# A pooled branch's output projection computed as seven half-size products, with its weight differences formed by GpSimd

## The reference, cut to what matters

```
u_a, z_a, q, k, v, o, z_b, gates, g_a, g_b = split(rms_norm(x) @ w_in)
mixed = groupwise(multiscale_pool(u_a)) @ pool_mix_w       # 4 groups of 256
y_a   = (mixed * pool_scale) * silu(z_a)                   # 512 x 1024
p_a   = y_a @ w_proj_pool                                  # 512 x 1024 x 1024, the product changed
merged = sigmoid(g_a + b_merge[0]) * p_a + sigmoid(g_b + b_merge[1]) * p_b
```

## Time and profile before

| | us |
|---|---|
| median of 3 runs (lowest, highest) | 1134.78 (1134.07, 1134.80) |
| the profiled execution's own time | 1134.12 |
| its span, first to last instruction | 1132.3 |
| TensorE busy | 1126.3 (99%), 6090 matmuls |
| VectorE busy | 724.7 (64%) |
| ScalarE busy | 614.6 (54%) |
| GpSimd busy | 197.0 (17%) |
| granted TensorE clock | 1.00 throughout |

### The profile page before, as it was taken

How to read it: one execution, slowest core, us unless ns; L and a number is a source line. 1 busy time by engine, 2 the same in 40 slices (tenths; PEclk the granted TensorE clock), 3 DMA queues, 4 the chain that set the end, 5 groups by cost and what they waited for, 6 DMA issues and landing times.

```text
span 1132.3 us, 15715 instructions
## 1 busy us (share of the span) xinstructions
PE 1126.3 (99%) x6090; PEld 935.0 (83%) x6090; DVE 724.7 (64%) x1222; ACT 614.6 (54%) x1062; POOL 197.0 (17%) x193
## 2 busy tenths in 40 slices
PE   9999999999999999999999999999999999999998
PEld 7888888888888888888889888777888888877877
DVE  5584534599845776534558667667786575666786
ACT  5533431243436676634246677777545587577752
POOL 1000135440000000000000002643503000706530
PEclk9999999999999999999999999999999999999999
DMA  6423476673331212233255523231254233222431
GB/s 195 133 75 112 124 247 233 218 244 100 122 112 57 93 58 73 76 127 112 75 204 156 130 86 76 74 92 58 95 186 132 76 111 104 75 75 76 147 124 74
DMA packets 115026, 134.13 MB, mean 118 GB/s; under 512 B 18620, under 2 KB 93756, under 8 KB 113416
## 3 DMA queue, kind: packets, MB, share of 16 engines
q1 hardware_dynamic: 113720, 128.93, 35.9%
q10 hardware_dynamic: 1232, 4.19, 1.0%
HBM read 120.37 MB, written 12.74 MB: 118 GB/s over the span
## 4 chain that ended last, share of the span: by engine, by line
PE 98%; ACT 1%; DMA 0%; DVE 0%; issue 0%; DVEq 0%; ACTq 0%
PE acc L2052 22%; PE acc L2053 22%; PE acc L2054 22%; PE aux L2052 3%; PE aux L2054 3%; PE aux L2053 3%; PE aux L2538 3%; PE aux L2526 3%; PE acc L2502 3%; PE acc L2451 2%; PE acc L2453 2%; PE acc L2452 2%; PE aux L2284 1%; PE aux L2286 1%; PE aux L2285 1%; PE aux L2144 1%
## 5 line engine op out<-in xcount | busy, mean ns | idle before, releaser
L2052 PE MATMUL acc<-ht_hi,whi 128*128 128x512 f32 x712 | 278.1, 391 | 0.0
L2054 PE MATMUL acc<-ht_hi,wlo 128*128 128x512 f32 x712 | 277.1, 389 | 0.0
L2053 PE MATMUL acc<-ht_lo,whi 128*128 128x512 f32 x712 | 277.1, 389 | 0.0
L1406 DVE TENSOR_TENSOR wlo<-raw,whi 128x2048 fp32r<-128x2048 f32 x68 | 159.5, 2346 | 101.8 <-ACT whi L951 95.6
L951 ACT ACTIVATE whi<-raw 128x2048 fp32r<-128x2048 f32 x68 | 129.9, 1910 | 56.8 <-DMA raw<-w_in_dram 22.1
L2052 PEld LDWEIGHTS acc<-ht_hi,whi 128*128 128x128 f32 x712 | 133.7, 188 | 28.1 <-DVE wlo L1406 0.6
L2054 PEld LDWEIGHTS acc<-ht_hi,wlo 128*128 128x128 f32 x712 | 133.6, 188 | 27.9
L2053 PEld LDWEIGHTS acc<-ht_lo,whi 128*128 128x128 f32 x712 | 133.7, 188 | 27.1
L848 POOL TENSOR_SCALAR whi<-raw 128x512 fp32r<-128x512 f32 x52 | 39.5, 760 | 621.9 <-DMA raw<-e_w_in_dram 464.6
L2052 PE MATMUL acc<-whi,ht_hi 128*128 128x512 f32 (+1 forms) x224 | 83.9, 375 | 0.0
L2054 PE MATMUL acc<-whi,ht_lo 128*128 128x512 f32 (+1 forms) x224 | 83.8, 374 | 0.0
(11 more groups left out here) (344 smaller groups left out, 2160.5 us busy)
## 6 DMA issues: line engine op xcount, KB each, us to landing
raw<-w_in_dram SPq DMA_DIRECT2D x72, 512.0 KB, 4.6
raw<-o_w_in_dram SPq DMA_DIRECT2D x28, 512.0 KB, 4.7
weight_terms<-term_parts SPq DMA_DIRECT2D x8, 1024.0 KB, 4.8
raw<-e_w_in_dram SPq DMA_DIRECT2D x14, 512.0 KB, 5.2
raw<-w_proj_pool_dram SPq DMA_DIRECT2D x8, 512.0 KB, 4.0
term_parts<-o_w_out_dram SPq DMA_DIRECT2D x8, 512.0 KB, 6.4
raw<-w_proj_mlstm_dram SPq DMA_DIRECT2D x8, 512.0 KB, 4.1
raw<-w_out_dram SPq DMA_DIRECT2D x8, 512.0 KB, 4.4
```

The costliest lines, as they stand in the source:

```text
L1406: v.tensor_tensor(wlo[:, slot, :], raw[:, slot, :], whi[:, slot, :].bitcast(F32), ALU.subtract).then_inc(w_split, 1)
L2052: mm(out_, w_hi_, x_hi, start=first, stop=False)
L2053: mm(out_, w_hi_, x_lo, start=False, stop=False)
L2054: return mm(out_, w_lo_, x_hi, start=False, stop=last)
```

## The change

The product p_a is computed by a seven-product scheme on halves: the contraction and the output channels are halved on the weights' side (blocks b11, b12, b21, b22 of 512x512) and the tokens and the contraction on the operand's side (`early` and `late` 256 tokens, tiles 0 to 3 and 4 to 7). The four weights T1 to T4 are differences of blocks, four subtractions by GpSimd per 128 rows, four batches; they are loaded, made and stored to DRAM while SyncE issues the loads of the za stage, and come back as one DMA of a megabyte each. The four operands' sums are made by VectorE with ScalarE during the ga stage. The stage has seven units, each of two banks by two groups by four tiles by three matmuls of 256 columns, in PSUM banks that keep partial sums from one unit to the next; ScalarE copies three of the partial results, VectorE adds them to others and multiplies by the gates. The loads and stores of the eight batches for the last projections move as well: the i of `between_loads` now counts from the first ga load, and the positions are given by `LOAD_AFTER`: batch 0 is loaded behind the load of ga's third unit, 1 behind the fourth, 2 behind pa's first; the store of batch 1 stands ahead of pa's second load, and the store of batch 2 ahead of its third (A12_B21); the other five batches stand between the loads of qk.

```diff
--- before.py
+++ after.py
@@ the Block's set-up @@
+        pool_weight_parts = at("pool_weight_parts", [P, 2, 4, WIDE], R4)
+        pool_terms_dram = nc.dram_tensor("pool_weight_terms", (4, P, 4, WIDE), F32, kind="Internal").ap()
...
-        for name, units, accs in (("gates", 1, 1), ("u", 4, 4), ("za", 4, 4), ("mix", 1, 4), ("ga", 4, 4), ("pa", 4, 4),
+        for name, units, accs in (("gates", 1, 1), ("u", 4, 4), ("za", 4, 4), ("mix", 1, 4), ("ga", 4, 4), ("pa", 7, 2),
...
+        POOL_OPERANDS = {A11_B11: (op_hi[:, 0:4, early], op_lo[:, 0:4, early]), S3_T3: (op_hi[:, 0:4, late], op_lo[:, 0:4, late]),
+                         A12_B21: (op_hi[:, 4:KT, early], op_lo[:, 4:KT, early]), S2_T2: (pool_sum_hi[1], pool_sum_lo[1]),
+                         S1_T1: (pool_sum_hi[0], pool_sum_lo[0]), S4_B22: (mix_parts[:, 0:4, early], mix_parts[:, 4:KT, early]),
+                         A22_T4: (op_hi[:, 4:KT, late], op_lo[:, 4:KT, late])}
+        def pool_bank(u, b):
+
+            if u == A12_B21:
+                return aux[:, b, :]
+            return acc[:, 2 * ((POOL_A + (u in (S3_T3, A22_T4))) % 2) + b, :]
@@ sync @@
-            stage("za", W1, COL_ZA)
+            pool_view = wview(A["w_proj_pool"][0])
+
+            def load_pool_parts(k):
+                if k == 0:
+                    sp.wait_ge(tr_lo, KT)
+                if k >= 2:
+                    sp.wait_ge(pool_terms_out[k % 2], 16)
+                for q, rows in ((0, k), (2, 4 + k)):
+                    sp.dma_start(pool_weight_parts[:, k % 2, q:q + 2, :].rearrange("p q c -> p (q c)"),
+                                 pool_view[:, rows, :]).then_inc(pool_parts_in[k % 2], 16)
+
+            def store_pool_terms(k):
+                sp.wait_ge(pool_terms_made, k + 1)
+                sp.dma_start(pool_terms_dram[:, :, k, :].rearrange("q p c -> p q c"),
+                             pool_weight_parts[:, k % 2, :, :]).then_inc(pool_terms_out[k % 2], 16)
+            for u in range(4):
+                load(W1, COL_ZA + u * UC, plan["za"][0] + u)
+                if u:
+                    store_pool_terms(u - 1)
+                load_pool_parts(u)
...
+            store_pool_terms(3)
...
+            LOAD_AFTER = (2, 3, 4, 11, 12, 14, 15, 17)
+
             def between_loads(i):
                 for b in range(len(BATCHES)):
-                    if 3 * b // 2 == i:
+                    if LOAD_AFTER[b] + 1 == i:
+                        store_terms(b)
+                for b in range(len(BATCHES)):
+                    if LOAD_AFTER[b] == i:
                         load_parts(b)
-                for b in range(len(BATCHES)):
-                    if 3 * b // 2 + 1 == i:
-                        store_terms(b)
-            stage("ga", W1, COL_GA)
-            between_loads(0)
             for u in range(4):
-                load(wview(A["w_proj_pool"][0]), u * UC, plan["pa"][0] + u)
-                between_loads(1 + u)
+                load(W1, COL_GA + u * UC, plan["ga"][0] + u)
+                between_loads(u)
+
+            def pool_term_weights(u, q):
+                n = POOL_N + u
+                slot_free(n)
+                sp.dma_start(raw[:, n % SLOTS, :], pool_terms_dram[q].rearrange("p k c -> p (k c)")).then_inc(w_loaded[n % SLOTS], 16)
+            load_wide(pool_view, 0, POOL_N + A11_B11, 0)
+            between_loads(4)
+            for stored_ in pool_terms_out:
+                sp.wait_ge(stored_, 32)
+            pool_term_weights(S3_T3, T3)
+            between_loads(5)
+            load_wide(pool_view, 0, POOL_N + A12_B21, 1)
+            pool_term_weights(S2_T2, T2)
+            pool_term_weights(S1_T1, T1)
+            load_wide(pool_view, WIDE, POOL_N + S4_B22, 1)
+            pool_term_weights(A22_T4, T4)
...
-                between_loads(5 + u)
+                between_loads(11 + u)
@@ gpsimd, ahead of the eight batches of term_parts @@
+            for k in range(4):
+                pool.wait_ge(pool_parts_in[k % 2], 32 * (k // 2 + 1))
+                b11, b12, b21, b22 = (pool_weight_parts[:, k % 2, q, :] for q in range(4))
+                step(nc.gpsimd.tensor_tensor(b11, b12, b11, ALU.subtract))
+                step(nc.gpsimd.tensor_tensor(b12, b22, b12, ALU.subtract))
+                step(nc.gpsimd.tensor_tensor(b22, b22, b11, ALU.subtract))
+                nc.gpsimd.tensor_tensor(b21, b21, b22, ALU.subtract).then_inc(pool_terms_made, 1)
@@ scalar @@
-                head(mixT[:, j, :], op_hi[:, j, :])
+                head(mixT[:, j, mix_cols(j)], op_hi[:, j, mix_cols(j)])
...
+            def heads_of_sums(u):
+                if u == 1:
+                    for m, (src, hi) in enumerate(((pool_sum_raw[0], pool_sum_hi[0]), (pool_sum_raw[1], pool_sum_hi[1]),
+                                                   (mixT[:, 0:4, late], op_hi[:, 0:4, late]),
+                                                   (mixT[:, 4:KT, early], mix_parts[:, 0:4, early]))):
+                        act.wait_ge(pool_sum, m + 1)
+                        nc.scalar.activation(hi[:, :, :], src[:, :, :], ACT.Copy).then_inc(pool_sum_high, 1)
+            stage("ga", mergedT, ACT.Sigmoid, ("b_merge", 0), heads_of_sums)
...
+            weight_heads(n0 + A12_B21)
+
+            def copies_of_term(u, part):
+                for b in range(2):
+                    act.wait_ge(pool_term, 2 * u + b + 1)
+                    nc.scalar.activation(pool_part[part][:, b, :], pool_bank(u, b), ACT.Copy).then_inc(pool_copied, 1)
+            copies_of_term(A11_B11, 0)
+            weight_heads(n0 + S2_T2)
+            copies_of_term(S3_T3, 1)
+            weight_heads(n0 + S1_T1)
+            copies_of_term(S2_T2, 2)
@@ vector @@
+            (a11, a21), (a12, a22) = ((mixT[:, tiles, early], mixT[:, tiles, late]) for tiles in (slice(0, 4), slice(4, KT)))
+            v.tensor_tensor(pool_sum_raw[0][:], a21, a22, ALU.add).then_inc(pool_sum, 1)
+            dve.wait_ge(pool_sum, 1)
+            v.tensor_tensor(pool_sum_raw[1][:], pool_sum_raw[0][:], a11, ALU.subtract).then_inc(pool_sum, 1)
+            v.tensor_tensor(a21, a11, a21, ALU.subtract).then_inc(pool_sum, 1)
+            dve.wait_ge(pool_sum, 3)
+            v.tensor_tensor(a12, a12, pool_sum_raw[1][:], ALU.subtract).then_inc(pool_sum, 1)
             weight_rests(n0 + 3)
+            for m, (src, hi, lo) in enumerate(((pool_sum_raw[0][:], pool_sum_hi[0][:], pool_sum_lo[0][:]),
+                                               (pool_sum_raw[1][:], pool_sum_hi[1][:], pool_sum_lo[1][:]),
+                                               (a21, op_hi[:, 0:4, late], op_lo[:, 0:4, late]),
+                                               (a12, mix_parts[:, 0:4, early], mix_parts[:, 4:KT, early]))):
+                dve.wait_ge(pool_sum_high, m + 1)
+                v.tensor_tensor(lo, src, hi.bitcast(F32), ALU.subtract).then_inc(pool_sum_split, 1)
...
+            weight_rests(n0 + S2_T2)
+            for b in range(2):
+                dve.wait_ge(pool_term, 2 * A12_B21 + b + 1)
+                ins, tiles = added(A12_B21, b, 0, 0)
+                step(ins)
+                gated(gates_of(0, early, b), tiles)
+            weight_rests(n0 + S4_B22)
+            for b in range(2):
+                dve.wait_ge(pool_term, 2 * S1_T1 + b + 1)
+                ins, tiles = added(S1_T1, b, 1, 1)
+                ins.then_inc(pool_added, 1)
+                dve.wait_ge(pool_added, b + 1)
+                gated(gates_of(1, late, b), tiles)
+            weight_rests(n0 + A22_T4)
+            for b in range(2):
+                dve.wait_ge(acc_ready, 2 * a0 + b + 1)
+                ins = gated(gates_of(1, early, b), two_tiles(pool_bank(S4_B22, b)))
+            ins.then_inc(acc_free, 1)
+            weight_rests(n0 + units)
...
@@ tensor @@
-            stage("pa", by_channels, op_hi, op_lo)
+
+            def pool_product(u, b):
+                slot, (hi, lo), bank = (POOL_N + u) % SLOTS, POOL_OPERANDS[u], pool_bank(u, b)
+                opens = u in (A11_B11, S3_T3, A12_B21)
+                for m in range(2):
+                    out_ = bank[:, UC * m:UC * m + UC]
+                    for k in range(4):
+                        c = WIDE * k + P * (2 * b + m)
+                        w_hi_, w_lo_ = whi[:, slot, c:c + P], wlo[:, slot, c:c + P]
+                        mm(out_, w_hi_, hi[:, k, :], start=opens and m == 0 and k == 0, stop=False, skip_group_check=True)
+                        mm(out_, w_hi_, lo[:, k, :], start=False, stop=False, skip_group_check=True)
+                        ins = mm(out_, w_lo_, hi[:, k, :], start=False, stop=m == 1 and k == 3, skip_group_check=True)
+                ins.then_inc(acc_ready if u in (S4_B22, A22_T4) else pool_term, 1)
+            for u in range(7):
+                wait_split(pe, POOL_N + u)
+                for b in range(2):
+                    if b == 0:
+                        if u == A11_B11:
+                            pe.wait_ge(acc_free, POOL_A - 1)
```

(57 more changed lines are left out.)

21 lines of the change are left out of this document (19 added, 2 removed).

## The result

| | before | after |
|---|---|---|
| time, median of 6 runs each on the same chip | 1134.78 us (1134.07 to 1135.28) | **1151.91 us** (1151.63 to 1152.87) |
| ratio to before, 95% interval | | 1.0155 [1.0144, 1.0166] |
| span of the profiled execution | 1132.3 | 1149.8 |

What follows compares the result with a forecast made beforehand. The prediction took TensorE, 98% of the chain, to bound the kernel. Its terms, -3.3 (product) + 4.0 (za) + 5.9 (queue) + 0.3 (rest of pa) + 1.5 (qk) = +8.4, gave 1142.6 us; interval 1132 to 1150.

Steps and rivals of the forecast that it cites:

- The product: In pa: 336 matmuls of 256 columns at 0.1198 us take 40.25 us against 43.52, so -3.3 us.
- The port in u and za: In u and za: GpSimd's subtractions delay VectorE, pausing TensorE 3.2 and 0.8 us; +4.0, bounds 0.9 to 7.
- SyncE's queue: At pa's third unit: its load stands behind waits for GpSimd's subtractions; pause of 5.9 us, bounds no pause to 9.8.
- qk: In the qk stage: more batches meet the convolutions and use up VectorE's margin; +1.5 us, between 0 and 4.8.
- The rest of pa: In pa's later units: loading and splitting fit their slots, except 0.3 us at S4_B22, the tightest.
- The fourth: In u, queue and qk: every subtraction holds VectorE for its full 1.29 us; +16, 1150 us, chance 0.10.
- Rivals 1 to 3: Subtractions fit gaps: 1131 to 1131.9, chance 0.13; queue absorbs u's delay: 1135.6, 0.09; u escapes, queue does not: 1138.0, 0.08.
- The fifth: In pa: wide weight loads fail to hide at 256 columns, so the stage isn't shorter; given no chance of its own.

Runs made afterwards that it cites:

- e3: Changed kernel without GpSimd's sixteen subtractions for the pooled projection and its 32 for the last two projections, transfers kept: 1130.86 us, ratio to before 0.9969.
- e1: Changed kernel without GpSimd's sixteen subtractions for the pooled projection's weights, loads and stores kept: 1145.56 us, ratio to before 1.0099.
- q1: Changed kernel, nothing left out, with T3's load moved ahead of batch 1's store and batch 2's load, and batch 2's store behind T2's load: 1143.81 us.
- p2: Kernel before the change with thirteen scratch additions on VectorE ahead of the weight rest of ga's last unit: 1145.41 us, ratio 1.0098.
- e2: Changed kernel without GpSimd's 32 subtractions of the eight batches for the last two projections, loads and stores kept: 1137.49 us, ratio to before 1.0028.
- p1: Kernel before the change with eight scratch additions on VectorE ahead of the weight rest of ga's last unit: 1136.67 us, ratio 1.0021.
- q2: Changed kernel with the pooled projection's subtractions begun after the third za unit's split, stores issued by GpSimd, parts 2 and 3 loaded behind ga's first load: 1146.01 us.
- q6: q4 with the eight batches' loads moved back near their places before the change, and batch 3 behind pa's last load: 1135.11 us, ratio to before 1.0007.
- q4: Changed kernel with pooled subtractions begun after the third za split, GpSimd issuing its own stores, and the eight batches spread over ga, pa and qk loads: 1137.03 us.

## Why the prediction was partly right

**The product: right.** -3.3 was forecast, from 336 x 0.1198 = 40.25; e3 lasts 40.31 and gains 3.4.

**The port in u and za: right in its mechanism and its length.** Forecast were no pause at the first za unit, 3.2 at the second and 0.8 at the third; the trace has 0.4, 3.45 and 1.0. What it left out is the lower clock behind the second pause, 1.8. The times hold as well: GpSimd started at 49.95 (49.4 forecast) and 65.29 (64.5), the second unit's rest ended at 77.05 (76.25). e1 showed that nothing but the subtractions was behind it, and VectorE's timeline that it was VectorE they delayed.

**SyncE's queue: right in its mechanism, near in its size.** The chain came much as written: from load to store it took 15.9, 17.2 and 13.8 us where 15.0, 16.6 and 16.1 were forecast, and the load of A12_B21 5.7 us into pa where 6.5 was forecast. From its load to its split that unit took 12.4 us (173.04 to 185.48) where 10.9 was taken from the earlier trace rows, since the transfer landed later. Its lateness was 6.65 us for 5.9 forecast. S3_T3's late megabyte made a pause of its own, 2.2 where "may be a microsecond late" was written, but it lay inside A12_B21's time, as the prediction said. This is read from the trace; no run takes away one of the two pauses alone. q1 showed that the order of the queue is behind both: 8.1 us. The upper bound was summed wrong: cycles of 16.1, 18.5 and 18 give a pause of 10.8 by the prediction's own terms, not 9.8, and three cycles may be no longer than 13.9 for no pause, not 14.2.

**A term was missing: the clock behind a pause.** "Any pause of TensorE that the change brings is lost in full" was as far as I went. In the trace three of the pauses have 5.0 us of slow matmuls behind them, and p2 shows the same in the kernel before. Of the 5.0, the 1.6 behind S3_T3's pause passed inside the wait for A12_B21, so 3.4 reached the span. Which pauses it falls behind is not fixed either: in e1 and q1 it falls behind qk's third pause too, where after has it at 1.00.

**qk: mis-sized, outside its bound.** This is the largest miss. 1.5 was forecast with 4.8 as the upper end; it measured 5.5 in four pauses and 5.8 from qk's start to the scores (e2 and q1 leave 6.3, with a fall of the clock in q1). The reason for taking little, "a TensorE already late gives VectorE time as well", did not hold. The reading of it, which no run tests, is that SyncE issues the batches behind slots that TensorE frees, so they are late with it and meet the same operations. VectorE's timeline shows two of the ways:

```profile
236.13 2.30 DVE L1514 TENSOR_TENSOR wlo<-raw,whi 128x2048 fp32r<-128x2048 f32 x1 [3.74 <-ACT whi L1036]
...
262.18 5.86 DVE L1740 SCALAR_TENSOR_TENSOR cacc<-cpad,vecs,cacc 128x512 f32<-128x512 f32 x4
...
272.55 2.28 DVE L1514 TENSOR_TENSOR wlo<-raw,whi 128x2048 fp32r<-128x2048 f32 x1
```

Ahead of the first pause VectorE was idle for 3.74: there the weights were late, their load standing in SyncE's queue behind a wait for GpSimd. Ahead of the rest at 272.55 it was not idle, and four of its operations took 5.86 where the earlier trace rows has 3.11 for four alone: the port. I had counted only the second way. How the 5.8 divide between the two was not measured. In the waits, SyncE (before 300 us) waits for GpSimd:

```profile
SPq L740 <- POOL term_parts L972: 85.7, 8, 13.9
SPq L707 <- POOL pool_weight_parts L965: 34.3, 4, 10.9
```

**The rest of pa** (0.3 at S4_B22) did not show.

**The sum as it should have been:** -3.2 + 4.9 (za) + 1.8 (clock in za) + 6.65 (A12_B21) + 1.6 (clock behind it) + 5.8 (qk) = +17.5, the span's own +17.5. Against the forecast's terms, qk is 4.3 too small, the clock's 3.4 are absent, za's and the queue's lengths are 0.9 and 0.75 too small, and the 0.3 did not come. The range was narrower than its own terms: all upper bounds together, as written, are -3.3 + 7 + 9.8 + 0.3 + 4.8 = +18.6, or 1152.7.

**The rivals.** The fourth, the fully locked port, comes nearest in time (1150), but not in its terms: it put the second za pause at 6.5, where 3.45 was measured, and cycles of 18 in the queue, where 15.9, 17.2 and 13.8 were. Rivals 1 to 3 each needed one of the two costs to be absent; both are there. The fifth fell with pa's 0.12 us.

## What to carry to other kernels

Where a saturated TensorE is given a pause, price the pause and what the clock may do behind it: here 1.6 to 1.8 us more behind each of three, and hardly anything behind six shorter ones, at 1.91 us and less of idle time. Then ask what the next unit waits for: slow matmuls ahead of a unit that is late by itself cost nothing, as those behind S3_T3's pause did. A store that waits for another engine's result, in the queue that also issues the loads, puts every load behind it at that engine's mercy; moving two calls was worth 8.1 of 17.1 us. Work on GpSimd is free only at its place: the same 32 subtractions cost at most some 0.5 us before and 14 after, so before moving such work, look at what VectorE does there and how much it has to spare.

## What the runs showed of the hardware

- The clock fell behind all eleven pauses of weight rests with 2.06 us or more of idle time in the profiled executions here (the shortest at 168.55 in e1, the longest p2's 9.16), and behind none with 1.72 (p1) or less. In between, length does not decide: it fell behind 1.86 (q2), 1.89 (q1) and 1.92 (e1) and stayed at 1.00 behind 1.89 (q6), 1.91 (after) and 1.95 (q4). Executions of the same kernel differ as well: q6 has five at a mean of 1.000 and six at 0.998, which are 1.8 us longer by their medians. What decides was not tested.
- While the clock is low, matmuls of 256 columns start 0.213 us apart instead of 0.12, and those of 512 columns 0.427 instead of 0.227 (after, from 177.13 and from 78.12).
- A VectorE operation of 16 elements took 1.15 us beside a GpSimd subtraction (51.95 to 53.10; GpSimd's lasted from 51.43 to 53.06), so the delay goes with GpSimd's instruction and not with the size of VectorE's. The Trainium skill (SBUF — State Buffer, SBUF: two separate sides) has the port pair that VectorE and GpSimd share locked for a whole instruction; the trace agrees for this one, and about for the one of 525 elements before it, which ended 0.55 after GpSimd's subtraction did and takes 0.71 alone. Where rival 4 went wrong was to put each subtraction's whole duration on top of VectorE's.
- 13 additions in a row on VectorE took 15.09 us in p2 where 13 x 0.73 = 9.5 was expected, with GpSimd's subtractions beside them.
- A DMA issued by GpSimd itself costs it 0.77 us and a further 0.3 of waiting for its own last result (q4), which lengthens each batch on an engine that has its own work.
